# A fused transformer block on one core: first modulation product in column groups, tokens by tile, constants in two parts

## What is computed

```python
c_act = jax.nn.silu(c)                       # c: 1 x 1024
mod = c_act @ w_mod[l] + b_mod[l]            # 1024 x 9216 weights, nine rows of 1024
sh1, sc1, ga1, sh2, sc2, ga2, sh3, sc3, ga3 = jnp.split(mod, N_MOD, axis=-1)
h = modulate(rms_norm(x, g_ffn1[l]), sh1, sc1)   # norm(x) * (1 + sc1) + sh1
x = x + 0.5 * (1 + ga1[:, None, :]) * swiglu(h, w1_gate[l], w1_up[l], w1_down[l])
```

## Time and profile before

| | us |
|---|---|
| median of 3 runs (lowest, highest) | 2987.6 (2987.29, 2990.9) |
| the profiled execution: its own time | 2986.41 |
| the profiled execution: its span | 2984.4 |
| first matmul of the first FFN (L691) after the span's start | 63.35 |
| PE busy over the span | 2598.4 (87%) |

### The profile page before, as it was taken

One profiled execution on the slowest core, in us unless ns is written; L12 is line 12 of the kernel. 1 busy time (PEld: TensorE's weight loads), 2 busy tenths in 40 slices (PEclk: granted clock), 3 DMA queues, 4 the chain that ended last, 5 costly groups with the idle time before them and its releaser, 6 DMA issues. The chain is left out here.

```text
span 2984.4 us, 25042 instructions
## 1 busy us (share of the span) xinstructions
PE 2598.4 (87%) x9163; PEld 1219.3 (41%) x9163; DVE 1047.0 (35%) x1220; ACT 452.3 (15%) x710; POOL 179.7 (6%) x458
## 2 busy tenths in 40 slices
PE   7999999988888999999999789688888888887884
PEld 2444444455555444444444445433333333333331
DVE  2555530233343133331011563423333333233334
ACT  2000000233212110000010222011111111111111
POOL 0000000000000000000000000011111111111111
PEclk9999999988889999999999789789899999899897
DMA  7444533011004011241221100199999999999995
GB/s 253 141 144 139 169 123 79 1 42 43 21 21 134 0 56 58 83 114 39 86 82 46 33 1 18 74 397 416 415 407 414 412 404 412 408 403 414 401 410 232
DMA packets 185705, 563.10 MB, mean 189 GB/s; under 512 B 16800, under 2 KB 132656, under 8 KB 160448
## 3 DMA queue, kind: packets, MB, share of 16 engines
q1 hardware_dynamic: 175264, 554.10, 48.7%
q0 software_dynamic: 10400, 8.42, 0.9%
HBM read 567.18 MB, written 20.97 MB: 197 GB/s over the span
## 5 line engine op out<-in xcount | busy, mean ns | idle before, releaser
L1073 PE MATMUL ps<-slot,xT 128*64 128x512 f32 x2048 | 518.8, 665 | 161.3 <-DMA slot<-in_expert_w_up 160.4
L691 PE MATMUL ps<-hT,slot 128*128 128x512 f32 x1408 | 614.0, 597 | 12.9 <-ACT hT L1160 7.2
L691 PEld LDWEIGHTS ps<-hT,slot 128*128 128x128 f32 x1408 | 267.3, 191 | 351.1 <-issue 348.6
L1073 PEld LDWEIGHTS ps<-slot,xT 128*64 128x64 f32 x2048 | 167.5, 153 | 510.6 <-issue 461.9
L719 PE MATMUL ps<-big,slot 128*128 128x512 f32 x704 | 310.0, 600 | 11.8 <-DVE big L1473 6.2
L1889 DVE COPY hT<-ps 128x256 f32<-128x256 f32 x64 | 27.2, 425 | 631.4 <-PE ps L1081 631.4
L1092 PE MATMUL ps<-slot,hT 128*64 128x512 f32 x1024 | 235.5, 602 | 1.2 <-DVE hT L1889 1.2
L1880 DVE RECIPROCAL xT<-xT 64x512 f32<-64x512 f32 x64 | 214.1, 3345 | 2.2
L719 PEld LDWEIGHTS ps<-big,slot 128*128 128x128 f32 x704 | 135.4, 193 | 182.0 <-issue 169.0
L1469 DVE RECIPROCAL eb<-eb 128x512 f32<-128x512 f32 x44 | 147.5, 3353 | 1.5
L1467 DVE TENSOR_SCALAR eb<-eb 128x512 f32<-128x512 f32 x44 | 18.8, 427 | 332.8 <-ACT eb L1170 332.8
(11 more groups left out here) (337 smaller groups left out, 2422.7 us busy)
## 6 DMA issues: line engine op xcount, KB each, us to landing
slot<-in_expert_w_gate SPq DMA_DIRECT2D x64, 2048.0 KB, 17.2
slot<-in_expert_w_up SPq DMA_DIRECT2D x64, 2048.0 KB, 22.6
slot<-in_expert_w_down SPq DMA_DIRECT2D x64, 2048.0 KB, 23.1
slot<-in_w_mod SPq DMA_DIRECT2D x18, 2048.0 KB, 8.0
slot<-in_w_gate SPq DMA_DIRECT2D x22, 1024.0 KB, 5.5
slot<-in_w_up SPq DMA_DIRECT2D x22, 1024.0 KB, 7.9
slot<-in_w_down SPq DMA_DIRECT2D x16, 1408.0 KB, 8.4
slot<-in_w_in SPq DMA_DIRECT2D x24, 512.0 KB, 5.8
```

The source lines that it names most:

```text
L691: last = mm(ps[:, 2 * j + g, :], w[:, g, k, j * P:(j + 1) * P], hT[:, k, META:TOK], start=(k == 0), stop=(k == KC - 1))
L1073: last = mm(ps[g * CAP:(g + 1) * CAP, j, :], xsT[j][:, k, :], w[g][:, k, :], start=(k == 0), stop=(k == KC - 1))
```

## The change

- The constants come in two parts. The first, 257 columns, holds `ident`, `ones` and a new column `quarters`, which is 1 on partitions 0, 32, 64 and 96 and 0 elsewhere. The rest of the constants, `bf` and `wf` are issued after the last modulation item of the first FFN, on a semaphore of their own (`s_late`) for which PE and DVE wait before the forgetting gate.
- x comes as four DMAs, a tile of 128 tokens each with a semaphore of its own. PE turns a tile into two banks as it comes; DVE copies tiles 0 and 2 to `xT`, ACT tiles 1 and 3. The engines no longer meet after this phase.
- The eight sums of squares stand ahead of the modulation product on PE. ACT loads the table of the square root before the squares, with a one-element activation, where it was loaded after them.
- The first four modulation items are loaded by rows: slot s holds the feature chunks 2s and 2s+1 with 2048 columns each, in pieces of 8 KB. `c_act` is repeated to 32 columns per chunk (`c_rep`), and a chunk's product goes to one of four groups of 32 columns of the array (`g`), so to 32 partitions of a bank: slots 0 and 2 use groups 0 and 32, slots 1 and 3 groups 64 and 96. 32 products remain 32 products.
- ACT and DVE copy two banks of 128 x 512 each, and 16 matmuls with `quarters` as the moving column add the four groups and turn the row, in place of the 16 transposes.

```diff
+             ("quarters", np.broadcast_to(p % 32 == 0, (P, 1)) * 1.0),
...
-        mod_row = big[0:1, 0:MOD_FIRST * 512]
+        mod_part = big[:, 0:MOD_FIRST * 512].rearrange("p (b n) -> p b n", b=MOD_FIRST)
+        c_rep = sb("c_rep", [P, KC, 32])
+        n_first = CONST["quarters"][0] + 1
...
-            sp.dma_start(cst[:, :], a["const"]).then_inc(s_in, 16)
-            sp.dma_start(cols[:, :], a["cols"]).then_inc(s_in, 16)
-            sp.dma_start(bf[:, :], a["b_f"].rearrange("a h -> h a")).then_inc(s_in, 16)
-            sp.dma_start(wf[:, :, :], w_in[:, :, 3072:3080]).then_inc(s_in, 16)
-            sp.dma_start(ring[5][:, :].rearrange("p (t d) -> p t d", t=4),
-                         a["x"][0].rearrange("(t p) d -> p t d", p=P)).then_inc(s_x, 16)
-            sp.dma_start(ring[4][0:META, 0:D], a["meta_tokens_2"]).then_inc(s_x, 16)
+            sp.dma_start(cst[:, 0:n_first], a["const"][:, 0:n_first]).then_inc(s_in, 16)
+            xin = ring[5][:, :].rearrange("p (t d) -> p t d", t=4)
+            for t in range(4):
+                sp.dma_start(xin[:, t, :], a["x"][0, t * P:(t + 1) * P, :]).then_inc(s_x[t], 16)
+                if t == 0:
+                    sp.dma_start(cols[:, :], a["cols"]).then_inc(s_cols, 16)
+            sp.dma_start(ring[4][0:META, 0:D], a["meta_tokens_2"]).then_inc(s_meta, 16)
...
             for s in range(MOD_FIRST):
-                mod_item(s, u.take(s, 1)[1], s)
+                sp.wait_ge(freed[s], u.take(s, 1)[1])
+                sp.dma_start(ring[s][:, :].rearrange("p (k n) -> p k n", k=2), w_mod[:, 2 * s:2 * s + 2, 0:MOD_FIRST * 512])\
+                    .then_inc(filled[s], 16)
...
                     mod_item(2, base2 + N_GU - 1, MOD_FIRST + N_GU - 1)
+                    sp.dma_start(cst[:, n_first:], a["const"][:, n_first:]).then_inc(s_late, 16)
+                    sp.dma_start(bf[:, :], a["b_f"].rearrange("a h -> h a")).then_inc(s_late, 16)
+                    sp.dma_start(wf[:, :, :], w_in[:, :, 3072:3080]).then_inc(s_late, 16)
...
-            pe.wait_ge(s_in, 64)
-            pe.wait_ge(s_x, 32)
+            pe.wait_ge(s_in, 16)
...
-            for k in range(KC):
-                for t in range(4):
-                    last = nc.tensor.transpose(ps[:, k, t * P:(t + 1) * P], xin[:, t, k * P:(k + 1) * P], ident)
+            for t in range(4):
+                pe.wait_ge(s_x[t], 16)
+                for k in range(KC):
+                    last = nc.tensor.transpose(ps[:, 2 * t + k // 4, k % 4 * P:(k % 4 + 1) * P], xin[:, t, k * P:(k + 1) * P], ident)
                 last.then_inc(s_tr, 1)
...
+            for n in range(KC):
+                norm_sum(0, n)
             pe.wait_ge(s_cact, 1)
             for s in range(MOD_FIRST):
                 pe.wait_ge(filled[s], u.take(s, 1)[0] + 16)
-                w = ring[s][:, :].rearrange("p (k n) -> p k n", k=KC)
-                for k in range(KC):
-                    last = mm(ps[0:1, 1 + s, :], c_act[:, k:k + 1], w[:, k, :], start=(k == 0), stop=(k == KC - 1))
+                w = ring[s][:, :].rearrange("p (k n) -> p k n", k=2)
+                for b in range(MOD_FIRST):
+                    for kk in range(2):
+                        g = 32 * (2 * (s % 2) + kk)
+                        last = mm(ps[g:g + 32, 4 + b, :], c_rep[:, 2 * s + kk, :], w[:, kk, b * 512:(b + 1) * 512],
+                                  start=(s < 2), stop=(s >= 2))
                 last.then_inc(freed[s], 1)
-                for n in range(3 * s, min(3 * s + 3, KC)):
-                    norm_sum(0, n)
             pe.drain().then_inc(s_mod, 1)
-            pe.wait_ge(s_mrow, 1)
+            pe.wait_ge(s_mrow, 2)
             for m in range(4 * MOD_FIRST):
-                last = nc.tensor.transpose(ps[:, 6, m:m + 1], mod_row[:, m * P:(m + 1) * P], ident[0:1, 0:1])
+                last = mm(ps[:, 1, m:m + 1], mod_part[:, m // 4, m % 4 * P:(m % 4 + 1) * P], const("quarters"), start=True, stop=True)
...
-            phase_end(act, 1)
+            for t in (1, 3):
+                act.wait_ge(s_tr, t + 1)
+                av(xT[:, :, META + t * P:META + (t + 1) * P],
+                   ps[:, 2 * t:2 * t + 2, :].rearrange("p b (k n) -> p (b k) n", k=4), ACT.Copy).then_inc(s_tro, 1)
+            act.wait_ge(s_trc, 2)
+            act.wait_ge(s_tro, 2)
+            phase_left(act, 1)
...
-                if r:
-                    av(fox_s[:, 15:16], eps_col[:, 0:1], ACT.Sqrt)
+                if r == 0:
+                    act.wait_ge(s_o, 1)
+                av(fox_s[:, 15:16], eps_col[:, 0:1], ACT.Sqrt)
...
-            av(mod_row.rearrange("p (b n) -> p b n", b=MOD_FIRST), ps[0:1, 1:1 + MOD_FIRST, :], ACT.Copy).then_inc(s_mrow, 1)
+            av(mod_part[:, 0:2, :], ps[:, 4:6, :], ACT.Copy).then_inc(s_mrow, 1)
...
+            v.tensor_copy(c_rep[:, :, :], c_act.unsqueeze(2).to_broadcast([P, KC, 32])).then_inc(s_cact, 1)
...
+            dve.wait_ge(s_mod, 1)
+            v.tensor_copy(mod_part[:, 2:4, :], ps[:, 6:8, :]).then_inc(s_mrow, 1)
             dve.wait_ge(s_mod, 2)
-            link(v.tensor_tensor(modT[:, 0:16], ps[:, 6, 0:16], col("b_mod")[:, 0:16], ALU.add))
+            link(v.tensor_tensor(modT[:, 0:16], ps[:, 1, 0:16], col("b_mod")[:, 0:16], ALU.add))
...
+            dve.wait_ge(s_late, 48)
```

More of the change, by code:

```diff
@@ L187, in build @@
         bf = sb("bf", [8, 1])
-        s_in = sem("inputs_in")
-        s_x = sem("x_in")
+        s_in = sem("first_constants_in")
+        s_cols = sem("columns_in")
+        s_late = sem("late_constants_in")
+        s_x = [sem(f"x_in{t}") for t in range(4)]
+        s_meta = sem("meta_in")
         filled = [sem(f"filled{s}") for s in range(N_SLOT)]
@@ L196, in build @@
         s_tr = sem("turned")
-        s_trc = sem("turned_copied")
+        s_trc = sem("even_tiles_turned_copied")
+        s_tro = sem("odd_tiles_turned_copied")
         s_cexp = sem("c_exp_ready")
@@ L629, in _ @@
                 pe.drain().then_inc(freed[s], 1)
-            pe.wait_ge(s_in, 64)
-            pe.wait_ge(s_x, 32)
+            pe.wait_ge(s_in, 16)
             xin = ring[5][:, :].rearrange("p (t d) -> p t d", t=4)
-            for k in range(KC):
-                for t in range(4):
-                    last = nc.tensor.transpose(ps[:, k, t * P:(t + 1) * P], xin[:, t, k * P:(k + 1) * P], ident)
+            for t in range(4):
+                pe.wait_ge(s_x[t], 16)
+                for k in range(KC):
+                    last = nc.tensor.transpose(ps[:, 2 * t + k // 4, k % 4 * P:(k % 4 + 1) * P], xin[:, t, k * P:(k + 1) * P], ident)
                 last.then_inc(s_tr, 1)
+            pe.wait_ge(s_meta, 16)
             pe.wait_ge(s_trc, 1)
             for k in range(KC):
-                last = nc.tensor.transpose(ps[:, 0, k * META:(k + 1) * META], ring[4][0:META, k * P:(k + 1) * P],
+                last = nc.tensor.transpose(ps[:, 1, k * META:(k + 1) * META], ring[4][0:META, k * P:(k + 1) * P],
                                            ident[0:META, 0:META])
@@ L643, in _ @@
                 pe.drain().then_inc(freed[s], 1)
-            phase_end(pe, 1)
+            phase_left(pe, 1)
             def norm_sum(r, n):
@@ L811, in _ @@
             phase_left(pe, 4)
+            pe.wait_ge(s_late, 48)
             for k in range(KC):
@@ L1132, in _ @@
             av = nc.scalar.activation
-            act.wait_ge(s_in, 64)
+            act.wait_ge(s_cols, 16)
             av(c_exp, col("c"), ACT.Exp, scale=-1.0).then_inc(s_cexp, 1)
-            phase_end(act, 1)
+            for t in (1, 3):
[5 more added lines that the diff above has]
+            phase_left(act, 1)
             def norm_std(r):
                 t0, t1 = HALVES[r][0][0], TOK
-                if r:
-                    av(fox_s[:, 15:16], eps_col[:, 0:1], ACT.Sqrt)
+                if r == 0:
+                    act.wait_ge(s_o, 1)
+                av(fox_s[:, 15:16], eps_col[:, 0:1], ACT.Sqrt)
                 for k in range(KC):
@@ L1411, in _ @@
             v.memset(eps_col[:, :], EPS).then_inc(s_o, 1)
-            for k in range(KC):
-                dve.wait_ge(s_tr, k + 1)
-                v.tensor_copy(xT[:, k, META:TOK], ps[:, k, :]).then_inc(s_trc, 1)
-            dve.wait_ge(s_tr, KC + 1)
-            v.tensor_copy(xT[:, :, 0:META], ps[:, 0, 0:KC * META].rearrange("p (k t) -> p k t", k=KC))
+            for t in (0, 2):
+                dve.wait_ge(s_tr, t + 1)
+                v.tensor_copy(xT[:, :, META + t * P:META + (t + 1) * P],
+                              ps[:, 2 * t:2 * t + 2, :].rearrange("p b (k n) -> p (b k) n", k=4)).then_inc(s_trc, 1)
             dve.wait_ge(s_cexp, 1)
@@ L1419, in _ @@
             link(v.reciprocal(c_exp, c_act))
-            v.tensor_tensor(c_act, c_exp, col("c"), ALU.mult).then_inc(s_cact, 1)
-            phase_end(dve, 1)
+            link(v.tensor_tensor(c_act, c_exp, col("c"), ALU.mult))
```

(4 more changed lines are left out.)

## The result

The changed kernel takes 2964.66 us (median of 4 runs, 2963.46 to 2967.29) against 2987.44 us before (median of 4, 2985.59 to 2990.9): a ratio of 0.9924, 95% interval 0.9906 to 0.9941. The profiled execution took 2963.49 us, its span 2961.1 us, 23.3 us shorter than before.

What follows compares the result with a forecast made beforehand. Bound: the chain to the first FFN's start, 63.35 us. Loads 5.3 and product 13.9, less table 1.5, `quarters` 2.4 and clock 1.6, with unsized terms, gave 19.0 us: 2967.4, plus 1.2, rounded 2968.5; range 2963 to 2976.

Steps and rivals of the forecast that it cites:

- the likeliest case: Whole kernel: the forecast of 2968.5 us, given 68%, with its own range of 2964.5 to 2972 us.
- A start is handed on: First FFN onward: PE is busy 315.8 of 320 us, so an earlier start of L691 shortens the whole time.
- The loads: Start: constants and small `wf` pieces leave x's way, 4.3 plus 1.0 us, so x's last tile lands near 9.1 us.
- From x to the sums: Start: transposes at 0.166 us end at 10.4 us; after copy and table load the first sum is at 13.65 us.
- The copies: Tile copies from PSUM, 128 x 1024: 1.0 us on ACT, 1.2 us on DVE, interpolated from other rows.
- The product: Modulation product: two column groups overlap, 64 records at 0.222 us take 14.2 us against 28.1, ending at 35.8 us.
- rival of four groups "where slots meet": Modulation product: four groups overlap, ending near 33.5 us; gain 21 to 22 us, time 2966 us; chance 4%.
- The weights: Modulation slots: the last lands near 31.5 us, its product starts at 32.3, leaving 0.8 us of slack.
- The tail: Between product and FFN: copies, then 16 `quarters` matmuls at 4.2 us in place of 1.15, then 1.4 us to L691.
- The clock: PE's clock halves after pauses or one-column work: 0.7 us at the tail, 0.9 us for the sums, 1.6 us together.
- earlier turning and copying: Start: part of the 19.0 us gain, from turning and copying x's tiles earlier; no size of its own.
- waits between the phases: Start: listed last in the sum that makes the 19.0 us gain; no size of its own.

Runs made afterwards that it cites:

- second trace: The changed kernel run again with nothing altered, beside later versions on one chip: 2965.69 us, ratio to before 0.993.
- fill-ins at the tail: Changed kernel plus three matmuls on constants, results unread, behind the modulation product and three behind the turning: 2963.4 us, one run.
- 7.41 with fill-ins: Changed kernel plus six matmuls on constants, results unread, in PE's pause ahead of the sums of squares: 2968.2 us, one run.

## Why the prediction was right

The time, 2964.7 us, lies just inside the likeliest case's own range (2964.5 to 2972), 3.8 us below the forecast of 2968.5; the gain was 22.8 us where 19.0 were forecast. Of the 3.8 us, 2.0 are the start of the FFN (42.33 against 44.3), and the rest is spread outside it. The size of the gain and its main cause, column groups that overlap, were right; how widely they overlap was not. By its own steps:

- **A start is handed on.** Right: 21.0 us at L707, 21.1 us at the experts.
- **The loads.** Mis-sized, within the bounds: the last tile of x landed at 10.5 us, not 9.1, so 3.8 us were gained and not 5.3. With the constants back in front it landed at 15.1, 4.6 us later. In the trace of the changed kernel the DMA rate was 283 to 348 GB/s between 5 and 8 us, not 426.
- **From x to the sums.** Mis-sized: transposes end at 12.28 instead of 10.4 us. Of these 1.9 us, 1.4 are the later landing. The rest is the rate: I took the mean of 0.166 us from 32 transposes. That mean hides two rates, 0.213 us for the first half and 0.109 for the second; in the changed kernel 27 of 32 ran at the slow one (distances between their starts). The median record shows it, 421 ns against 300 before. The first line is of the kernel before, the second of the changed one (least/median/most):

```profile
L635 PE MATMUL ps<-cst,slot x32: 272/300/448, 15.7 to 20.7; 128*128 128x128 f32 x32
```

```profile
L647 PE MATMUL ps<-cst,slot x32: 272/421/476, 4.8 to 12.0; 128*128 128x128 f32 x32
```

- **The copies.** Right: 1.02 us on ACT and 1.23 on DVE, as interpolated; the table load stood on the path as forecast, with 1.28 us. From the last transpose to the first sum it took 3.3 us, as forecast.
- **The product.** The mechanism was right and the size off: 8.89 us, not 14.2. The step that failed is the two-wide rate, "The new loop order alternates between two groups as well (g and g + 32 within a slot), not among four". It is true within a slot, but where slots meet four groups run. PE's weight loads show it in the changed kernel: two per 0.43 us step first, and then six, four, four when slot 1 joins slot 0's last four steps.

```profile
26.85 0.12 PEld L675 LDWEIGHTS ps<-slot,c_rep 128*32 128x32 f32 x2 [0.31 <-issue]
27.28 0.12 PEld L675 LDWEIGHTS ps<-slot,c_rep 128*32 128x32 f32 x2 [0.31 <-issue]
27.71 0.15 PEld L675 LDWEIGHTS ps<-slot,c_rep 128*32 128x32 f32 x6 [0.31 <-issue]
28.14 0.15 PEld L675 LDWEIGHTS ps<-slot,c_rep 128*32 128x32 f32 x4 [0.28 <-issue]
```

The single records of the same trace show that these are slot 1's: its first weight load, the one behind the wait for `filled[1]`, and its first matmul start at 27.72 us, and slot 0's last matmul, the one that signals `freed[0]`, starts at 29.00.

Eight steps a slot, four of them shared with the next, make 20 steps of 0.43 us or 8.6 us. This was my rival of four groups "where slots meet", which I gave 4% against the loop order. Its time, 2966, is nearer to the measured one than my own forecast, and its gain of 21 to 22 us is what L707 shows (21.0); it deserved far more. What "TensorEngine Tiling (Array Packing)" of the Trainium skill allows in "Theoretical Speedup", up to 4x at 32 columns, the trace bears out nearly in full, with 3.8x: 0.114 us a record with four groups in turn, against 0.43 with one. The loss by slow weight loads that the prediction weighed did not come: a load of 32 columns took 0.11 us of each 0.43 us step.

- **The weights.** Nearly bound, as forecast: the fourth slot, issued at 6.6 us, landed 23.9 us later at 30.5, 0.7 us before the changed kernel reached it at 31.2. In its second trace it came first and waited, until 31.6. The same loads landed at 30.5 to 32.0 from run to run; why they differ is open.
- **The tail.** The turning took 4.65 us, not 4.2: at full clock it takes 3.63, as the kernel with fill-ins at the tail shows, and the half clock on its end added 1.0.
- **The clock.** Right in kind, and the price of a fall in the sums, which I put at 1.6 to 2.4 us with a chance of one in two, was 1.6 to 1.8 in nine other traces and 3.0 in this one (7.41 with fill-ins, 10.46 without). The 0.9 in the sum is half of one fall, and a fall came in every trace without fill-ins there. The FFN is reached at 42.33, against 42.7 by the terms without clock and 44.3 with it, and the fall across its start cost it about as much as before: 326.7 us to the down weights against 326.6.

The errors nearly cancel, and the forecast is right partly for that reason: the first sum came 1.9 us late (15.57 against 13.65), the sums took 2.5 us more (10.46 against 7.9), the product 5.3 us less, the copies and the turning 0.6 us more. That leaves 0.4 us between 42.7 and 42.33, and against the 44.3 with the clock's 1.6 us, 2.0 us. The sum also leaves a size unexplained: its terms with a number make 13.7 of the 19.0 us, and the 5.3 left to "earlier turning and copying" and "waits between the phases" have none of their own. x in one piece shows that turning by tile is worth 2.7 us at the end of the product.

## What to carry to other kernels

In this kernel the product had one column on its stationary side (the operand that is loaded as weights). Giving its accumulations or its column blocks to four groups of 32 columns turned 28 us into 9, and into 7 where four groups stand in turn. Once that is done, read what lands last: here the weights bound each further gain at PE. A mean over few instructions can hide two clock levels, so look at least, median and most before using it elsewhere; and the half clock is a cost of its own behind short pauses, which unread matmuls took away ahead of the sums, but not around the 16 one-column matmuls of the turning. Last, a start that moves by less than a microsecond can be given back behind it: two kernels reached the FFN 0.5 and 0.7 us earlier and its first down matmul no earlier.

## What the runs showed of the hardware beyond this

- The granted clock in the rows does not fit the durations at the very start: it reads 1.00 from 0 on, while 128 x 128 transposes took 0.213 us each up to 11.5 us in the changed kernel, up to 19.0 in the kernel before and up to 15.9 with x in one piece, and 0.109 us from there on. PE's first work in these kernels, wherever it began (4.8, 15.7 and 9.8 us), ran at half speed.
- Matmuls do not start in program order when they go to other column groups: slot 1's first started at 27.72 us, when six records of slot 0, which stands ahead of it, had not begun and two had just begun. So the program need not alternate group by group; how far ahead PE can reach in other orders was not run.
- The clock also fell with PE busy, each time behind a run of one-column matmuls: at 39.7 us with fill-ins on both sides, and at 514 us in the kernel before, behind 24 one-column records. With fill-ins of 256 columns in the pause ahead of the sums it stayed at 1.00. The falls differ in place and length from kernel to kernel (3.4 or 6.8 us long in the sums, 6.8 or 10.2 at the tail), so the same turning took 3.6 to 6.3 us, and a single trace of one kernel should not be read finer than that. Why the clock fell at 16.5 us behind a pause of 1.3 us, and not at 23 us in the kernel before behind one of 1.6 us, stays open.
